# Unequal token halves in the up and input projections, and a separate read of the bias columns

## The reference, cut to what matters

```python
h = rms_norm(x, g) * (1.0 + mods[:, 3*j+1, None]) + mods[:, 3*j, None]
ffn:   silu(h @ w1) * (h @ w3) @ w2        # 1024 -> 2816 -> 1024
mixer: z = h @ w_in                        # 1024 -> 2464, then attention and retention, then @ w_out
x = x + coef * mods[:, 3*j+2, None] * rms_norm(o, g)
```

## Time and profile before

| | |
|---|---|
| median of 3 runs | 2462.67 us (2459.4 to 2465.18) |
| profiled execution, its own time | 2464.77 us |
| span of its trace | 2463.0 us |
| TensorE (PE) matmuls busy | 2317.2 us, 94%, 17536 of them |
| VectorE (DVE) busy | 1261.2 us, 51% |
| ScalarE (ACT) busy | 806.7 us, 33% |
| GpSimd (POOL) busy | 912.4 us, 37% |
| mean granted TensorE clock | 0.976 of full |

### The profile page before, as it was taken

One profiled execution on the slowest core, in us unless ns is written; L12 is line 12 of the kernel. 1 busy time (PEld: TensorE's weight loads), 2 busy tenths in 40 slices (PEclk: granted clock), 3 DMA queues, 4 the chain that ended last, 5 costly groups with the idle time before them and its releaser, 6 DMA issues.

```text
span 2463.0 us, 43818 instructions
## 1 busy us (share of the span) xinstructions
PE 2317.2 (94%) x17536; PEld 2187.7 (89%) x17536; DVE 1261.2 (51%) x1882; ACT 806.7 (33%) x1329; POOL 912.4 (37%) x400
## 2 busy tenths in 40 slices
PE   1999999999889999999999999999988999999997
PEld 1999999899647899999989999998974599999996
DVE  7433369868273433337253333997835515333551
ACT  2322232333334522223242223224342544222321
POOL 1433334434112533334443333344431144333343
PEclk9999999999899999999999999999998899999998
DMA  6222258522210122226312223782230022222551
GB/s 232 75 87 85 86 186 282 193 78 77 79 35 26 61 85 85 85 92 249 129 61 85 85 85 120 259 282 80 82 112 16 20 69 69 85 85 85 190 197 60
DMA packets 71794, 273.00 MB, mean 111 GB/s; under 512 B 8672, under 2 KB 10080, under 8 KB 70816
## 3 DMA queue, kind: packets, MB, share of 16 engines
q1 hardware_dynamic: 71712, 271.88, 32.4%
HBM read 268.40 MB, written 3.45 MB: 110 GB/s over the span
## 4 chain that ended last, share of the span: by engine, by line
PE 74%; DVE 11%; issue 8%; POOL 2%; ACT 2%; DMA 2%; DVEq 0%; SPq 0%; POOLq 0%; ACTq 0%
PE ps L565 21%; PE ps L569 21%; PE ps L566 21%; POOL w_lo L469 2%; DVE ret_q L1466 1%; DVE ret_k L1466 1%; PE ps L575 1%; PE ps L613 1%; DMA raw<-in_w_mix 1%; DVE wide_v L1356 1%; DVE wide_v L1315 1%; PE ps L906 1%; PE ps L879 1%; PE ps L873 1%; PE ps L930 1%
## 5 line engine op out<-in xcount | busy, mean ns | idle before, releaser
L469 POOL TENSOR_TENSOR w_lo<-raw,w_hi 128x1024 fp32r<-128x1024 f32 (+1 forms) x304 | 788.0, 2592 | 1325.7 <-ACT w_hi L993 1002.5
L565 PE MATMUL ps<-h_hi,w_hi 128*128 128x274 f32 x3296 | 897.9, 290 | 4.9 <-DVE z_tmp L1435 4.9
L566 PE MATMUL ps<-h_lo,w_hi 128*128 128x274 f32 x3296 | 898.8, 290 | 0.0
L569 PE MATMUL ps<-h_hi,w_lo 128*128 128x274 f32 x3296 | 690.6, 291 | 0.0
L565 PEld LDWEIGHTS ps<-h_hi,w_hi 128*128 128x128 f32 x3296 | 626.7, 190 | 6.3 <-issue 6.2
L566 PEld LDWEIGHTS ps<-h_lo,w_hi 128*128 128x128 f32 x3296 | 621.0, 188 | 0.2
L993 ACT CAST w_hi<-raw 128x1024 fp32r<-128x1024 f32 (+1 forms) x236 | 268.2, 1136 | 880.6 <-PE ps L569 693.0
L569 PEld LDWEIGHTS ps<-h_hi,w_lo 128*128 128x128 f32 x3296 | 521.0, 188 | 0.0
L565 PE MATMUL ps<-u_hi,w_hi 128*128 128x272 f32 x1408 | 381.9, 290 | 11.1 <-POOL w_lo L469 10.9
L566 PE MATMUL ps<-u_lo,w_hi 128*128 128x272 f32 x1408 | 381.6, 290 | 0.0
L1315 DVE CUSTOM_DVE_ANT_0 wide_v<-ada_w,ps 128x1024 bf16<-128x1024 f32 x288 | 332.3, 1217 | 47.2 <-DMA ada_w<-in_ada 28.8
(11 more groups left out here) (239 smaller groups left out, 2398.6 us busy)
## 6 DMA issues: line engine op xcount, KB each, us to landing
raw<-in_w_up SPq DMA_DIRECT2D x176, 512.0 KB, 3.3
ada_w<-in_ada SPq DMA_DIRECT2D x160, 512.0 KB, 4.4
raw<-in_w_dn SPq DMA_DIRECT2D x64, 704.0 KB, 4.6
raw<-in_w_mix SPq DMA_DIRECT2D x64, 512.0 KB, 3.4
decay<-in_decay SPq DMA_DIRECT2D x2, 2048.0 KB, 8.2
x<-in_x SPq DMA_DIRECT2D x1, 2176.0 KB, 8.8
rope_tab<-in_rope SPq DMA_DIRECT2D x2, 1088.0 KB, 4.9
out_y<-x SPq DMA_DIRECT2D x1, 2176.0 KB, 6.6
```

The costliest lines, as they stand in the source:

```text
L469: pool.tensor_tensor(w_lo[:, slot, 0:width], raw[:, slot, 0:width], w_hi[:, slot, 0:width].bitcast(F32), ALU.subtract).then_inc(lo_done.se ...
L565: pe.matmul(ps[:, bank + t, 0:half], wh, hi[:, n], start=start, stop=False)
L566: pe.matmul(ps[:, bank + t, 0:half], wh, lo[:, n], start=False, stop=False)
L569: last = pe.matmul(ps[:, bank + t, 0:half], wl, hi[:, n], start=False, stop=stop)
```

## The change

The token halves of the `h` rows are no longer equal. The first has `HT` = 272 columns, the second `HB` = 276: 272 tokens and the four bias columns. Rows of `h_hi` and `h_lo` grow from 548 to `HP` = 560 columns (2240 bytes), of which the last twelve are not used. VectorE multiplies only the 544 token columns by `rinv`, and copies the four bias columns out of PSUM with an operation of its own behind it, which now raises the signal. `wide_rinv` loses its four columns and its name.

```diff
-HW = TW // 2
+HB = TW - HT
+HP = T + 16
...
-        wide_rinv = sb("wide_rinv", [P, TW])
-        rinv = wide_rinv[:, 0:T]
+        rinv = sb("rinv", [P, T])
...
-            [("h_hi", [P, KD, TW], F32R), ("h_lo", [P, KD, TW], F32R)],
+            [("h_hi", [P, KD, HP], F32R), ("h_lo", [P, KD, HP], F32R)],
...
-        def wide_pair(b):
-            return ps[:, b:b + 2, 0:HW]
+        def biases(b):
+            return ps[:, b + 1, HT:HB]
...
-            def tile3(bank, slot, kk, hi, lo, start, stop, half=HT):
+            def tile3(bank, slot, kk, hi, lo, start, stop, second=HT):
...
+                width = (HT, second)
                 for t in range(2):
-                    n = slice(t * half, (t + 1) * half)
-                    pe.matmul(ps[:, bank + t, 0:half], wh, hi[:, n], start=start, stop=False)
-                    pe.matmul(ps[:, bank + t, 0:half], wh, lo[:, n], start=False, stop=False)
+                    n = slice(t * HT, t * HT + width[t])
+                    pe.matmul(ps[:, bank + t, 0:width[t]], wh, hi[:, n], start=start, stop=False)
+                    pe.matmul(ps[:, bank + t, 0:width[t]], wh, lo[:, n], start=False, stop=False)
...
-                        last = tile3(4 * f + 2 * w, w, k, h_hi[:, k, :], h_lo[:, k, :], k == 0, k == KD - 1, HW)
+                        last = tile3(4 * f + 2 * w, w, k, h_hi[:, k, :], h_lo[:, k, :], k == 0, k == KD - 1, HB)
...
-            v_.memset(wide_rinv[:, T:TW], 1.0).then_inc(filled.sem, 1)
...
-                        v_.tensor_tensor(halves(wide_s[:, f, :]), wide_pair(4 * f), halves(wide_rinv[:, :]), ALU.mult)\
-                            .then_inc(up_out.sem, 1)
+                        v_.tensor_tensor(halves(tmp_s[:, f, :]), pair(4 * f), halves(rinv[:, :]), ALU.mult)
+                        v_.tensor_copy(wide_s[:, f, T:TW], biases(4 * f)).then_inc(up_out.sem, 1)
...
-                    v_.tensor_tensor(halves(z_tmp[:, z % 2, :]), wide_pair(bank), halves(wide_rinv[:, :]), ALU.mult)\
-                        .then_inc(z_mul.sem, 1)
+                    v_.tensor_tensor(halves(z_tmp[:, z % 2, 0:T]), pair(bank), halves(rinv[:, :]), ALU.mult)
+                    v_.tensor_copy(z_tmp[:, z % 2, T:TW], biases(bank)).then_inc(z_mul.sem, 1)
```

More of the change, by code:

```diff
@@ L557, in _ @@
                     pe.matmul(ps[:, 2 * n + k, 0:P], ones[:, :], ones[:, :], start=True, stop=True).then_inc(sig.sem, 1)
-            def tile3(bank, slot, kk, hi, lo, start, stop, half=HT):
+            def tile3(bank, slot, kk, hi, lo, start, stop, second=HT):
                 wh = w_hi[:, slot, kk * P:(kk + 1) * P]
                 wl = w_lo[:, slot, kk * P:(kk + 1) * P]
+                width = (HT, second)
                 for t in range(2):
-                    n = slice(t * half, (t + 1) * half)
-                    pe.matmul(ps[:, bank + t, 0:half], wh, hi[:, n], start=start, stop=False)
-                    pe.matmul(ps[:, bank + t, 0:half], wh, lo[:, n], start=False, stop=False)
+                    n = slice(t * HT, t * HT + width[t])
+                    pe.matmul(ps[:, bank + t, 0:width[t]], wh, hi[:, n], start=start, stop=False)
+                    pe.matmul(ps[:, bank + t, 0:width[t]], wh, lo[:, n], start=False, stop=False)
                 for t in range(2):
-                    n = slice(t * half, (t + 1) * half)
-                    last = pe.matmul(ps[:, bank + t, 0:half], wl, hi[:, n], start=False, stop=stop)
+                    n = slice(t * HT, t * HT + width[t])
+                    last = pe.matmul(ps[:, bank + t, 0:width[t]], wl, hi[:, n], start=False, stop=stop)
                 return last
@@ L600, in first_tiles @@
                             pe.wait_ge(lo_done.sem, lo_done.at(l, chunk + w + 1))
-                        for t in range(2):
-                            n = slice(t * HW, (t + 1) * HW)
-                            pe.matmul(ps[:, 2 * w + t, 0:HW], w_hi[:, w, k * P:(k + 1) * P], h_hi[:, k, n],
+                        for t, w_t in enumerate((HT, HB)):
+                            n = slice(t * HT, t * HT + w_t)
+                            pe.matmul(ps[:, 2 * w + t, 0:w_t], w_hi[:, w, k * P:(k + 1) * P], h_hi[:, k, n],
                                       start=k == 0, stop=False)
-                            pe.matmul(ps[:, 2 * w + t, 0:HW], w_lo[:, w, k * P:(k + 1) * P], h_hi[:, k, n],
+                            pe.matmul(ps[:, 2 * w + t, 0:w_t], w_lo[:, w, k * P:(k + 1) * P], h_hi[:, k, n],
                                       start=False, stop=False)
@@ L610, in first_tiles @@
                             pe.wait_ge(h_ready.sem, h_ready.at(l, H_AT[j] + 2 + 2 * k + 2))
-                        for t in range(2):
-                            n = slice(t * HW, (t + 1) * HW)
-                            last = pe.matmul(ps[:, 2 * w + t, 0:HW], w_hi[:, w, k * P:(k + 1) * P], h_lo[:, k, n],
+                        for t, w_t in enumerate((HT, HB)):
+                            n = slice(t * HT, t * HT + w_t)
+                            last = pe.matmul(ps[:, 2 * w + t, 0:w_t], w_hi[:, w, k * P:(k + 1) * P], h_lo[:, k, n],
                                              start=False, stop=k == KD - 1)
@@ L701, in z_tile @@
                     for k in range(KD):
-                        last = tile3(bank, slot, k, h_hi[:, k, :], h_lo[:, k, :], k == 0, k == KD - 1, HW)
+                        last = tile3(bank, slot, k, h_hi[:, k, :], h_lo[:, k, :], k == 0, k == KD - 1, HB)
                     last.then_inc(w_used.sem, 1)
@@ L1388, in ffn @@
                         dve.wait_ge(w_used.sem, w_used.at(l, FFN_C[s] + i * 4 + 2 * f + 1))
-                        v_.tensor_tensor(halves(wide_s[:, f, :]), wide_pair(4 * f), halves(wide_rinv[:, :]), ALU.mult)\
-                            .then_inc(up_out.sem, 1)
+                        v_.tensor_tensor(halves(tmp_s[:, f, :]), pair(4 * f), halves(rinv[:, :]), ALU.mult)
+                        v_.tensor_copy(wide_s[:, f, T:TW], biases(4 * f)).then_inc(up_out.sem, 1)
                         dve.wait_ge(up_lo.sem, up_lo.at(l, n - 1))
                         dve.wait_ge(w_used.sem, w_used.at(l, FFN_C[s] + i * 4 + 2 * f + 2))
-                        v_.tensor_tensor(halves(wide_v[:, f, :]), wide_pair(4 * f + 2), halves(wide_rinv[:, :]), ALU.mult)\
-                            .then_inc(up_out.sem, 1)
+                        v_.tensor_tensor(halves(tmp_v[:, f, :]), pair(4 * f + 2), halves(rinv[:, :]), ALU.mult)
+                        v_.tensor_copy(wide_v[:, f, T:TW], biases(4 * f + 2)).then_inc(up_out.sem, 1)
                         dve.wait_ge(up_silu.sem, up_silu.at(l, 2 * n + 2))
```

2 lines of the change are left out of this document (1 added, 1 removed).

## The result

The changed kernel takes 2444.09 us (median of 4 runs, 2441.91 to 2449.52), against 2463.93 us for the kernel before on the same chip: ratio 0.9914, with a 95% interval from 0.9892 to 0.9936. Run again later, it took 2448.84 us against 2463.72 us, 0.9941 [0.9922, 0.996]. The forecast was 2448 us.

A forecast was written before the change was run, and what follows sets the result against it. TensorE was taken to bound the kernel, by matmul count times distance between starts. Faster matmuls on `h` (-16.8 us) and copies (+1.3) gave -15.5 us, forecast 2448 us; range 2438 to 2467, the likeliest case's own 2444 to 2454.

The forecast's parts named there:

- The pace on `h`: Matmuls reading `h`: 127.9 ns falls to a mean of 126.1, 1.8 ns less on 9312 matmuls, 16.8 us saved.
- The pace on `u`: Down projections: matmuls of 272 columns stay at 125.3 ns; the prediction is wrong if this moves at all.
- three features: `h` rows: second half 1096 bytes in (not 16's multiple), rows 2192 apart (not 64's), halves not multiples of four columns; excess 1.8 ns.
- tile 2: Input projection tile at 126.3 ns a matmul with unchanged shape, read as a sign that the 1.8 ns is avoidable.
- The copies: VectorE's four-column copies from PSUM: 0.08 us each, 16 counting in the mixer, 1.3 us added; not held up by GpSimd.
- The mixer's stretch: Where VectorE sets the pace: 768 matmuls save nothing, and the wait for `z_tmp` grows from 4.9 to 7 to 8 us.
- The sum: Whole kernel: -16.8 us from matmuls and +1.3 from copies, -15.5 us together.
- the 192 matmuls of L613: First tiles: taken to follow each other closely, so counted among the 9312 matmuls that save 1.8 ns each.
- A: Matmuls on `h`: half the excess stays, 276 columns cost today's 127.9 ns, 1.3 ns saved; 2452 us, chance 17%.
- B: Matmuls on `h`: more than the excess goes, both halves cost 125.3 ns, 2.6 ns saved; 2440 us, chance 8%.
- C: Matmuls on `h`: pace doesn't depend on where a half begins, only copies count; 2464 to 2467 us, chance 20%.
- D: Matmuls on `u`: starts 32 bytes off 64 add an 18th 64-byte piece, 1.8 ns each; 2473 us, chance 12%.

## Why the prediction was right

*The pace on `h`.* Forecast 1.8 ns less, 6.05 us for 48; measured 127.89 to 126.11, 1.78 ns. By form, the first halves went to 125.16 (forecast 125.3) and the second to 127.05 (127.0). 9312 x 1.78 = 16.6 us, where the prediction had 16.8. The pace on `u`, which should not move at all, didn't: 125.28 and 125.29 ns. The groups by form of the changed kernel have the 9888 in two widths, and one width for `u`, as the earlier trace rows had one each:

```profile
L567 PE MATMUL ps<-h_hi,w_hi 128*128 128x276 f32 x1648 | 478.8, 291 | 0.0
L567 PE MATMUL ps<-h_hi,w_hi 128*128 128x272 f32 x1648 | 476.1, 289 | 7.7 <-DVE z_tmp L1437 7.7
...
L567 PE MATMUL ps<-u_hi,w_hi 128*128 128x272 f32 x1408 | 380.5, 289 | 10.1 <-POOL w_lo L470 10.1
```

The prediction left the cause among three features. The runs show two of them at work: starts off a multiple of 16 bytes, and the row spacing, which it named but didn't separate. The third, a width that isn't a multiple of four columns, is supported by one run and spoken against by another. That the excess would go whole was an inference from tile 2. In the kernel before, four tiles of 206 ran at 126.3 to 126.5 ns, tiles 2 and 4 of either input projection, and all others at 127.8 to 128.1, though their addresses and widths are the same. Those four look like the second pace that the kernel with the spacing alone shows in 63 tiles, and why a tile has the one or the other is open. So tile 2 showed that 274 columns can run at 126.4, and not that better addresses bring it about.

The size came out to 0.02 ns, and that is in part luck. The spacing alone gave 0.91 ns and the halves alone 1.22, a split that the prediction had no term for, and the distance between `h_hi` and `h_lo`, also no term of it, would have taken 0.83 ns of the 1.78 back had it been 32 bytes longer. The 0.42 ns for a column rest on rows whose last digit is 0.01 us in six matmuls, 1.7 ns for one; at full clock the changed kernel has 127.05 - 125.16 for four columns, 0.47 ns for one.

*The copies.* Groups of VectorE by form, and the row of `z_tmp` by line (durations min/median/max in ns), in the changed kernel:

```profile
L1390 DVE TENSOR_TENSOR wide_s<-ps,rinv 128x544 f32<-128x544 f32 x88 | 63.8, 724 | 15.0 <-PE ps L571 13.8 <-DVE rinv L1380 1.0
L1391 DVE COPY wide_s<-ps 128x4 f32<-128x4 f32 x88 | 13.3, 151 | 0.0
```

```profile
L1437 DVE COPY z_tmp<-ps x42: 144/151/152, 500.6 to 1811.8; 128x4 f32<-128x4 f32 x42
```

0.15 us each and never held up, with GpSimd busy 37% of the time: the reading of the earlier trace rows held. In the mixer a rotary operation with two sources in SBUF stands right behind a copy, while GpSimd splits weights (timelines of VectorE and GpSimd):

```profile
576.14 0.15 DVE L1437 COPY z_tmp<-ps 128x4 f32<-128x4 f32 x1
576.21 2.21 DVE L1467 TENSOR_TENSOR ret_q<-wide_s 32x544 f32<-32x544 f32 x1
...
575.04 2.82 POOL L470 TENSOR_TENSOR w_lo<-raw,w_hi 128x1024 fp32r<-128x1024 f32 x1 [5.64 <-ACT w_hi L988]
```

The copy out of PSUM takes its 0.15 us inside GpSimd's operation; the rotary operation takes 2.21 us, three times the 0.71 to 0.72 us of the next three like it, and ends 0.56 us behind GpSimd's. By the rule of the Trainium skill (SBUF — State Buffer, the section on two separate sides) the trace agrees again. The multiplication became 4 ns shorter (728 to 724). In the mixer's stretch the timeline of VectorE shows what the copies cost:

```profile
572.26 0.72 DVE L1436 TENSOR_TENSOR z_tmp<-ps,rinv 128x544 f32<-128x544 f32 x1
...
585.92 0.72 DVE L1436 TENSOR_TENSOR z_tmp<-ps,rinv 128x544 f32<-128x544 f32 x1
...
599.57 0.72 DVE L1436 TENSOR_TENSOR z_tmp<-ps,rinv 128x544 f32<-128x544 f32 x1
```

A block of two tiles takes 13.66 and 13.65 us, and 13.45 before; 0.10 us a copy, where 0.08 was forecast: 16 x 0.10 = 1.6 us instead of 1.3.

*The mixer's stretch collects nothing.* Waits of TensorE in the changed kernel (us in total, times, longest), against the earlier trace rows:

```profile
PE ps L605 <- ACT h_hi L1018: 61.1, 8, 51.4
...
PE ps L567 <- DVE z_tmp L1437: 7.7, 6, 1.3
```

4.9 became 7.7 us; forecast 7 to 8. Its longest is seen at the matmul that the earlier trace rows showed with 0.91 (timeline of TensorE):

```profile
600.49 0.39 PE L567 MATMUL ps<-h_hi,w_hi 128*128 128x272 f32 x1 [1.29 <-DVE z_tmp L1437]
```

*The sum.* Forecast -15.5 us, span -15.3, both profiled at a clock of 0.976. Counted from the measured side, all 9888 matmuls at 1.78 ns are 17.6 us less and the wait for `z_tmp` is 2.8 us more, 14.8 us together. One small term was wrong: the 192 matmuls of L613 don't follow each other closely. Their starts are 192 ns apart in the mean before and 191 after, so they gave under 0.1 us and not 0.35.

*Rivals.* A (276 columns as dear as 274 were) fell: 127.05 against 128.82 for the second halves. Its rule, a price in steps of four columns, may still hold in part (274 and 276 cost the same on `u`); what it missed is that the 274 columns also paid for their start and spacing. B fell, since 276 columns do cost more than 272. C fell: the pace does depend on where a half begins. Its argument that addresses aren't the whole cause stands, by the two paces of the kernel with the spacing alone. The distance that the Trainium skill gives (TensorE: Matmul & The Clock Gate, Part 1), columns by clock plus about 2.5 ns, has no term for an address and so none for the difference between the kernels with rows 8 and 16 bytes later, 128.61 and 126.13; the trace disagrees. D fell at once, with `u` at 125.3 from a start 32 bytes past a multiple of 64, and the runs put its boundary at 16 bytes: its mechanism works for a move of 8 bytes, as the kernel with `h` 8 bytes later shows (1.0037), though at a higher price than its 1.8 ns.

*What stays open.* Why spacing 2192 costs on `h` and not on `u`; why a wider first half that overlaps the second costs more than its columns and slows the second too; why the distance between high and low parts acts with opposite signs; and why the same instructions on the same addresses have two paces. These are 0.5 to 2 ns a matmul. Together they suggest that something about how the successive reads of TensorE fall against each other counts, but no run here tests that.

## What to carry to other kernels

Where the time is the number of matmuls times the distance of their starts, read that distance, per operand, from rows far apart: two loops that should be equal and aren't by 2 ns were worth 15 us here. Start every moving slice on a multiple of 16 bytes, rows included; then measure the spacing, the widths and the distance between the parts instead of assuming them, over all tiles and not over one, since one kernel can have two paces. A tiny read of PSUM of its own is 0.1 us where its engine sets the pace and nothing elsewhere, and spreading that engine's order evenly took away a wait of 7.7 us, which the faster matmuls had lengthened.

## What was not expected of the hardware

Eight bytes of start address cost 2.5 ns in 126 for a matmul of 272 or 276 columns in fp32r, and 4 or 8 bytes cost 3.1 and 3.5 ns in 125.3 on the other operand (2.1 ns for 8 bytes with rows 2192 bytes apart); 16 or 32 bytes cost nothing. One loop ran the same instructions on the same addresses at 127.1 ns in three of its four stages and at 126.4 in the other. A gap of 32 bytes between two tensors that are read in turn changed the pace by -0.5 and +0.8 ns. And the mean granted clock of an execution moves its span without any change of the kernel: that before has 2465.4 to 2468.2 us at 0.974 and 2454.7 to 2458.2 us at 0.98, some 10 us, more than half of what this change is worth.
